# Split weights of a transformer kernel at 160 instead of 192 modulo 256 bytes

## The chip, the cores and the metric

One core of a Trainium2 chip runs the whole program. The metric is the device time of one execution in microseconds; three runs of the kernel before gave a median of 2162.12 us (2159.3 to 2169.41).

## The reference

The reference applies two blocks to one sequence of 256 tokens with 1024 features, all in fp32. The first block has two layers, each a mixer and a convolutional feed-forward part, with RMS norms around both:

```python
x = x + rmsnorm(mixer(rmsnorm(x)))            # layer 0: SSD scan, layer 1: RG-LRU
h = rmsnorm(x, norm_ffn_pre[i])
f = conv_ffn(h, w_up, conv_w, conv_b, w_down)  # 1024 -> 8192 -> gelu(g) * v -> 1024
x = x + rmsnorm(f, norm_ffn_post[i])
```

The second block has two layers of differential attention and a gated delta rule in both directions, merged by gates, and then an MLP with squared ReLU (1024 to 4096 to 1024). Its scales, shifts and gates come from one vector, c, times a matrix of 1024 x 6144 per layer (the "ada" weights). The result must agree with fp32 arithmetic.

## The kernel before

**Layout and tiling.** Activations lie transposed, features on the 128 partitions and the 256 tokens along the free dimension, so every large product has a 128x128 weight matrix as stationary operand and 256 columns of activations as moving operand. All large weights are packed on the host into one stream, w_in, of 263 chunks of 128 x 2048 fp32 (1 MB). A chunk of kind a gives two output tiles of one "unit" (8 matrices each, accumulated over the 1024 inputs); a chunk of kind b takes two input tiles into the 8 accumulators of acc.

**Splitting.** To keep fp32 precision with the fast fp32r format, each weight w is split into w_hi (its rounded copy) and w_lo = w - w_hi, each activation likewise (h_hi and h_lo, or mv_hi and mv_lo). Three products replace one: w_hi * h_hi, w_hi * h_lo, w_lo * h_hi (function three, L484 to L486). ScalarE makes w_hi from raw, half a chunk (128x1024) at a time (act_split, L461); VectorE makes w_lo (dve_split, L468). There are two w_hi and two w_lo tiles, chosen by the parity of the chunk, and three raw tiles.

**Order.** SyncE loads chunk c into raw[c % 3] once chunk c - 3 is split. act_split for a half waits for the load and until TensorE has finished the half that last lay there (semaphore half_done); dve_split waits for act_split (high_parts), and TensorE waits for dve_split (chunk_split). Each half is 24 matmuls, each chunk 48, so 263 chunks are 526 halves and 12624 matmuls. The rest of the program runs between chunks: the stages are, in order, ssd_in (20 chunks), the SSD scan, ssd_out (8), ffn0 (48), lru_in (10), the RG-LRU, lru_out (5), ffn1 (48), and then twice in2 (14), gates (8) with the attention, the delta rule, bra and brb (2 each), out2 (4) and mlp (32). pe_norm (L380) sums squares with fp32 matmuls. The delta rule's fp32 matmuls (L1743 to L1824) work on tiles in ada_ring, tmp, keep and h. In the ffn stages pe_ada (L1318) puts one block of 8 ada products, 384 columns wide, ahead of each chunk of kind b; its results go to misc[0] and misc[1] in turn, and its weights come through two slots of ada_ring, loaded from POOL's queue.

**Memory.** Every tile in SBUF is allocated in order, 128 partitions by so many bytes, each start rounded to 32 bytes. In order and in bytes per partition: raw0 to raw2, x, h, h_hi, h_lo (8192 each), mv_hi, mv_lo (4096 each), par (10088), con (12432), ada_ring (24576), ada_turned (1536), ada_cols (1536), rstd (1024), tmp (4096), cact (32), fold_r (128), ident_r, neg_up_r, cs_parts (512 each), mod (384), gsc (128), keep (43008), weights_offset (128), and then w_hi0, w_hi1, w_lo0, w_lo1 (8192 each). weights_offset is never read or written. With it, w_hi0 starts at 192 modulo 256 bytes; as all four weight tiles are 8192 bytes long, so do the others, and so does every one of the eight 512-byte matrices in a half.

late is a second view of the same bytes: it is allocated at the place of w_hi0 and released at once, so w_hi and w_lo lie over its first 8192 elements. Its 10240 elements hold the SSD scan's tiles while no weights are split (xdt, xdtd, btok, cb, e, e2, st, tok), and its last 2048 elements, above the weights, hold lru_out's w8, attention's rot and the delta rule's kt and vt.

Of the kernel before, what the change touches and what calls it, by code (L numbers as in the profile page):

```python
# [25 lines left out]
P = 128  # L26
# [232 lines left out]
def build(nc, x_in, w_in, gates_in, ada_in, par_in, con_in, out):  # L259
# [7 lines left out]
    with ctx:  # L267
        def sb(name, shape, dtype=f32):
            return ctx.enter_context(nc.sbuf_tensor(name, shape, dtype))
# [32 lines left out]

        keep_cols, late_cols = 10752, 10240
        keep = sb("keep", [P, keep_cols])
        sb("weights_offset", [P, 32])
        with nc.sbuf_tensor("late", [P, late_cols], f32) as late:
            pass
        w_hi = [sb(f"w_hi{i}", [P, CW], f32r) for i in range(2)]
# [1970 lines left out]
```

## Time and profile before

| | us |
|---|---|
| median of three runs | 2162.12 (2159.3 to 2169.41) |
| the profiled execution | 2163.65, of which the profile's span is 2162.0 |
| TensorE busy, matmuls | 1986.0 (92%), 15973 records |
| TensorE busy, weight loads | 1874.7 (87%) |
| VectorE busy | 1339.4 (62%) |
| ScalarE busy | 1010.2 (47%) |
| DMA | 154 GB/s over the span |
| mean granted TensorE clock | 0.953 of full speed |

How to read it: a matmul is recorded from its issue to its end, and several are in flight, so records overlap. The time from one start to the next is the pace of the stream, and the record's own length (276 to 285 ns) is not. In the names of a group, the tile left of the arrow is written, the first one right of it is the moving operand and the second one the stationary operand. An fp32 matmul leaves two records, an fp32r matmul one.

### The profile page before, as it was taken

How to read it: one execution, taken by the hardware profiler on the slowest of the kernel's cores; microseconds unless marked ns; L12 is line 12 of the kernel's file. 1: busy time of each engine (PE TensorE's matmuls, PEld its weight loads, DVE VectorE, ACT ScalarE, POOL GpSimd, SP SyncE). 2: the span in 40 equal slices, each digit the busy share in tenths (PEclk: the TensorE clock that was granted, in tenths of full speed). 3: DMA queues.
4: the chain of work that ended last, by engine and by line, in shares of the span. 5: the costliest groups of instructions: out<-in, count | busy, mean ns of one | idle time of the engine just before them, and what ended most of it. 6: DMA issues, size and time to landing. Idle time of an engine off the chain costs nothing.

```text
span 2162.0 us, 39527 instructions
## 1 busy us (share of the span) xinstructions
PE 1986.0 (92%) x15973; PEld 1874.7 (87%) x15973; DVE 1339.4 (62%) x2017; ACT 1010.2 (47%) x1490; POOL 17.2 (1%) x36
## 2 busy tenths in 40 slices
PE   7989989999896799999799999889989998988998
PEld 6977979999785699999689888889988898888998
DVE  5836576776574676667567655555555765555555
ACT  5644555555457455555455520344445552034443
POOL 0000000000000000000000000000000000000000
PEclk9997999999987899999899999999999999999999
DMA  7530447667532267676233400235543340023553
GB/s 281 181 117 1 176 175 262 256 257 257 210 136 85 98 244 262 262 261 229 83 131 145 154 1 1 98 126 192 191 173 117 137 157 20 1 79 117 195 192 120
DMA packets 43885, 333.98 MB, mean 154 GB/s; under 512 B 4864, under 2 KB 4992, under 8 KB 5504
## 3 DMA queue, kind: packets, MB, share of 16 engines
q1 hardware_dynamic: 38592, 277.89, 35.3%
q0 software_dynamic: 4608, 50.33, 6.3%
q10 hardware_dynamic: 576, 4.19, 0.5%
q8 instruction: 82, 1.34, 0.2%
q14 instruction: 27, 0.22, 0.0%
HBM read 331.35 MB, written 1.05 MB: 154 GB/s over the span
## 4 chain that ended last, share of the span: by engine, by line
PE 84%; DVE 9%; ACT 5%; issue 2%; DMA 0%; DVEq 0%; ACTq 0%
PE unit L484 14%; PE unit L485 14%; PE unit L486 14%; PE acc L484 8%; PE acc L485 7%; PE acc L486 7%; PE misc L380 2%; PE acc L1778 2%; PE misc L1318 2%; PE unit L1771 2%; PE misc L1782 2%; DVE w_lo L468 1%; ACT w_hi L461 1%; PE acc L1381 1%; DVE tmp L1562 1%
## 5 line engine op out<-in xcount | busy, mean ns | idle before, releaser
L468 DVE TENSOR_TENSOR w_lo<-raw,w_hi 128x1024 fp32r<-128x1024 f32 x526 | 640.4, 1225 | 483.8 <-ACT w_hi L461 473.6
L461 ACT ACTIVATE w_hi<-raw 128x1024 fp32r<-128x1024 f32 x526 | 555.1, 1060 | 676.0 <-PE unit L486 404.3
L484 PE MATMUL unit<-h_hi,w_hi 128*128 128x256 f32 x2656 | 756.2, 285 | 47.1 <-DVE h_lo L395 32.4
L485 PE MATMUL unit<-h_lo,w_hi 128*128 128x256 f32 x2656 | 748.0, 282 | 0.0
L486 PE MATMUL unit<-h_hi,w_lo 128*128 128x256 f32 x2656 | 747.7, 282 | 0.0
L484 PEld LDWEIGHTS unit<-h_hi,w_hi 128*128 128x128 f32 x2656 | 512.1, 193 | 57.2 <-issue 40.9
L485 PEld LDWEIGHTS unit<-h_lo,w_hi 128*128 128x128 f32 x2656 | 510.4, 192 | 0.2
L486 PEld LDWEIGHTS unit<-h_hi,w_lo 128*128 128x128 f32 x2656 | 509.0, 192 | 0.0
L484 PE MATMUL acc<-mv_hi,w_hi 128*128 128x256 f32 x1360 | 386.3, 284 | 36.3 <-DVE mv_lo L540 36.3
L485 PE MATMUL acc<-mv_lo,w_hi 128*128 128x256 f32 x1360 | 381.8, 281 | 0.0
L486 PE MATMUL acc<-mv_hi,w_lo 128*128 128x256 f32 x1360 | 381.5, 281 | 0.0
L484 PEld LDWEIGHTS acc<-mv_hi,w_hi 128*128 128x128 f32 x1360 | 260.9, 192 | 57.0 <-DVE mv_lo L540 38.2
L485 PEld LDWEIGHTS acc<-mv_lo,w_hi 128*128 128x128 f32 x1360 | 260.5, 192 | 0.0
L486 PEld LDWEIGHTS acc<-mv_hi,w_lo 128*128 128x128 f32 x1360 | 259.3, 191 | 0.0
L380 PE MATMUL misc<-h,con 128*128 128x256 f32 x192 | 64.2, 505 | 36.9 <-ACT h L367 36.7
L380 PEld LDWEIGHTS misc<-h,con 128*128 128x128 f32 x192 | 48.9, 262 | 50.4 <-ACT h L367 30.4
L1847 ACT ACTIVATE h<-acc 128x512 f32<-128x512 f32 x4 | 2.4, 597 | 169.8 <-PE acc L1800 169.8
L536 ACT ACTIVATE mv_hi<-keep 128x512 fp32r<-128x512 f32 x93 | 57.4, 619 | 41.6 <-DVE keep L934 13.5
L540 DVE TENSOR_TENSOR mv_lo<-keep,mv_hi 128x512 fp32r<-128x512 f32 x93 | 63.5, 687 | 14.5 <-ACT mv_hi L536 14.2
L990 ACT ACTIVATE keep<-unit,par 128x256 f32<-128x256 f32 x128 | 64.2, 550 | 0.0
L1771 PE MATMUL unit<-ada_ring,keep 128*128 128x128 f32 x384 | 53.8, 296 | 9.1 <-DVE ada_ring L1910 9.1
L1043 DVE SCALAR_TENSOR_TENSOR keep<-unit,par,keep 128x254 f32<-128x254 f32 x128 | 55.8, 478 | 8.4
(311 smaller groups left out, 2038.8 us busy)
## 6 DMA issues: line engine op xcount, KB each, us to landing
raw<-w_in SPq DMA_DIRECT2D x263, 1024.0 KB, 4.8
ada_ring<-ada_in POOLq DMA_DIRECT2D x32, 1536.0 KB, 8.5
con<-con_in ACTq DMA_DIRECT2D x1, 1424.0 KB, 6.5
keep<-gates_in ACTq DMA_DIRECT2D x1, 1280.0 KB, 5.6
par<-par_in ACTq DMA_DIRECT2D x1, 1261.0 KB, 14.8
x<-x_in SPq DMA_DIRECT2D x1, 1024.0 KB, 5.9
out<-x SPq DMA_DIRECT2D x4, 256.0 KB, 2.3
con<-con_in ACTq DMA_DIRECT2D x1, 130.0 KB, 6.0
```

The source lines that it names most:

```text
L380: last = mm(misc[0][:, 0:T], ones, h[:, t, :], start=(t == 0), stop=(t == 7))
L461: act(half(w_hi, c, k), raw[c % RAW][:, CW // 2 * k:CW // 2 * (k + 1)], ACT.Copy).then_inc(S("high_parts"), 1)
L468: tt(half(w_lo, c, k), raw[c % RAW][:, CW // 2 * k:CW // 2 * (k + 1)], half(w_hi, c, k).bitcast(f32), ALU.subtract).then_inc(S("chunk_spli ...
L484: mm(out, w, m, start=first, stop=False)
L485: mm(out, w, ml, start=False, stop=False)
L486: return mm(out, wl, m, start=False, stop=last)
L536: act(mv_hi[:, b % 2, :, :], src, ACT.Copy).then_inc(S("mv_hi_done"), 1)
L540: tt(mv_lo[:, b % 2, :, :], src, mv_hi[:, b % 2, :, :].bitcast(f32), ALU.subtract).then_inc(S("mv_ready"), 1)
L990: ins = act(fc[:, s], unit[u % 2][:, s], ACT.Identity, bias=column(u, 4 * side + 3, i), scale=column(u, 4 * side + 2, i))
L1043: ins = stt(fc[:, o + 2:o + T], src[:, o:o + T - 2], column(u, 4 * side, i), fc[:, o + 2:o + T], ALU.mult, ALU.add)
L1318: ins = mm(misc[n % 2][g:g + 32, 0:ADA_W], cact[:, k:k + 1].to_broadcast([P, 32]), ada_slot[n % 2][:, k, :], start=(k < 4), stop=(k >= 4))
L1771: ins = mm(unit[c][:, P * hd:P * (hd + 1)], W["lt"][:, c, hd, :], W["t"][:, c, hd, :], start=True, stop=True)
```

## The change

The spacer ahead of late and the weights becomes 24 instead of 32 elements per partition, 96 instead of 128 bytes. w_hi0, w_hi1, w_lo0, w_lo1 and late start 32 bytes lower, at 160 modulo 256 bytes. Nothing else is different.

```diff
@@ -302,7 +302,7 @@
 
         keep_cols, late_cols = 10752, 10240
         keep = sb("keep", [P, keep_cols])
-        sb("weights_offset", [P, 32])
+        sb("weights_offset", [P, 24])
         with nc.sbuf_tensor("late", [P, late_cols], f32) as late:
             pass
         w_hi = [sb(f"w_hi{i}", [P, CW], f32r) for i in range(2)]
```

## Rows read from the trace of the kernel before

**Rows 1.** The page, part 4: the chain that ended last, by engine and by line.

```profile
PE 84%; DVE 9%; ACT 5%; issue 2%; DMA 0%; DVEq 0%; ACTq 0%
PE unit L484 14%; PE unit L485 14%; PE unit L486 14%; PE acc L484 8%; PE acc L485 7%; PE acc L486 7%; PE misc L380 2%; PE acc L1778 2%; PE misc L1318 2%; PE unit L1771 2%; PE misc L1782 2%; DVE w_lo L468 1%; ACT w_hi L461 1%; PE acc L1381 1%; DVE tmp L1562 1%
```

**Rows 2.** The page, part 5: costliest groups of instructions (columns named in the line above).

```profile
L468 DVE TENSOR_TENSOR w_lo<-raw,w_hi 128x1024 fp32r<-128x1024 f32 x526 | 640.4, 1225 | 483.8 <-ACT w_hi L461 473.6
L461 ACT ACTIVATE w_hi<-raw 128x1024 fp32r<-128x1024 f32 x526 | 555.1, 1060 | 676.0 <-PE unit L486 404.3
L484 PE MATMUL unit<-h_hi,w_hi 128*128 128x256 f32 x2656 | 756.2, 285 | 47.1 <-DVE h_lo L395 32.4
...
L484 PE MATMUL acc<-mv_hi,w_hi 128*128 128x256 f32 x1360 | 386.3, 284 | 36.3 <-DVE mv_lo L540 36.3
```

**Rows 3.** The waits: engine, tile, line, whom it waited for, us, times, longest.

```profile
ACT w_hi L461 <- PE unit L486: 404.3, 275, 8.9
ACT w_hi L461 <- PE acc L486: 270.4, 159, 5.8
...
PE acc L484 <- DVE mv_lo L540: 36.3, 7, 21.0
PE unit L484 <- DVE h_lo L395: 32.4, 16, 4.7
```

**Rows 4.** Timeline of TensorE in ssd_in: start us, us, engine, line, instruction.

```profile
56.25 0.28 PE L484 MATMUL unit<-h_hi,w_hi 128*128 128x256 f32 x1
...
59.08 0.28 PE L484 MATMUL unit<-h_hi,w_hi 128*128 128x256 f32 x1
```

**Rows 5.** Timeline of TensorE in mlp_0, the same columns.

```profile
1481.02 0.28 PE L486 MATMUL acc<-mv_hi,w_lo 128*128 128x256 f32 x1
1481.13 0.28 PE L484 MATMUL unit<-h_hi,w_hi 128*128 128x256 f32 x1
...
1483.85 0.28 PE L484 MATMUL unit<-h_hi,w_hi 128*128 128x256 f32 x1
```

**Rows 6.** Windows: busy us and records of each engine, clock, DMA share, GB/s.

```profile
core 0: us, PE busy (x) PEld busy (x) DVE busy (x) ACT busy (x) POOL busy (x), PEclk, DMA share, GB/s
60.00:80.00 20.00, 20.00 (x172) 20.00 (x171) 17.80 (x29) 13.65 (x24) 0.00 (x0) 1.00 0.48 166
...
331.00:347.00 16.00, 16.00 (x139) 15.49 (x142) 10.84 (x17) 7.59 (x10) 0.00 (x0) 1.00 0.77 287
351.00:363.00 12.00, 12.00 (x108) 12.00 (x108) 7.88 (x12) 6.86 (x9) 0.00 (x0) 1.00 0.76 292
1460.00:1600.00 140.00, 140.00 (x1237) 140.00 (x1237) 78.83 (x78) 68.28 (x79) 0.00 (x0) 1.00 0.54 191
```

**Rows 7.** One line's instructions (L1782, L1749): ns min/median/max.

```profile
L1782 PEld LDWEIGHTS misc<-tmp,ada_ring x320: 192/192/333, 1263.6 to 1896.8; 128*128 128x128 f32 x160
L1782 PE MATMUL misc<-tmp,ada_ring x320: 274/275/421, 1263.8 to 1896.9; 128*128 128x128 f32 x160
...
L1749 PE MATMUL misc<-keep x64: 275/275/275, 1245.4 to 1858.6; 128*128 128x128 f32 x64
```

**Rows 8.** The same view of L1844, L1436 (ScalarE) and L901 (VectorE).

```profile
L1844 ACT ACTIVATE ada_ring<-ada_ring x8: 1040/1042/1057, 1252.0 to 1804.2; 128x1024 f32<-128x1024 f32 x8
...
L1436 ACT ACTIVATE h<-h x8: 1041/1052/1061, 1115.5 to 1726.9; 128x1024 f32<-128x1024 f32 x8
...
L901 DVE TENSOR_TENSOR late<-late x8: 1217/1224/1226, 160.1 to 206.3; 128x1024 f32<-128x1024 f32 x8
```

**Rows 9.** Timelines of ScalarE and VectorE in mlp_0, with the idle time before.

```profile
1462.29 1.06 ACT L461 ACTIVATE w_hi<-raw 128x1024 fp32r<-128x1024 f32 x1 [1.14 <-PE unit L486]
1465.01 1.06 ACT L461 ACTIVATE w_hi<-raw 128x1024 fp32r<-128x1024 f32 x1 [1.66 <-PE unit L486]
...
1463.39 1.23 DVE L468 TENSOR_TENSOR w_lo<-raw,w_hi 128x1024 fp32r<-128x1024 f32 x1 [0.89 <-ACT w_hi L461]
```

**Rows 10.** Timeline of TensorE in in2_0, an fp32 group of 256 columns.

```profile
1109.57 3.62 PE L1381 MATMUL acc<-h,con 128*128 128x256 f32 x16
```

## The prediction

> **What bounds the kernel now.** I read the chain that ended last first. TensorE holds 84% of it, and 64% of the span (14 + 14 + 14 + 8 + 7 + 7) lies on the three lines that multiply by the split weights [rows 1]. The costliest groups say the same: 2656 matmuls of each of three kinds into unit and 1360 of each into acc, beside 526 half-chunk splits on ScalarE (L461) and 526 on VectorE (L468) [rows 2]. Both splitters wait for TensorE or for each other, not TensorE for them: ScalarE waited 404.3 + 270.4 us for matmuls, VectorE 473.6 us for ScalarE [rows 2], and the largest waits of a matmul for the other engines are 32 to 36 us each, at stage starts [rows 3]. So the time moves if a matmul's pace moves, and hardly otherwise.
>
> Then I read the timeline of TensorE for that pace, and it has two. In ssd_in, 24 starts from 56.25 to 59.08 us are 117.9 ns apart [rows 4]. In mlp_0, 24 starts from 1481.13 to 1483.85 us are 113.3 ns apart [rows 5]. The granted clock is 1.00 at both, the shapes and tiles are the same. From the starts in ns the paces are 117.78 and 113.33; the difference of 4.44 ns is the price I use. The reader can find it again in the windows [rows 6]: 20 us hold 172 matmul records at the slow pace (two of them cut by the edges: 20 / 170 = 117.6 ns), 140 us hold 1237 at the quick one (140 / 1235 = 113.4 ns).
>
> A stretch keeps its pace from beginning to end and changes it only after an interruption. Counting the timeline by half chunks of 24 matmuls, 517 of 526 can be read (the others are at the half clock): 199 slow, 318 quick. Slow are 20 halves of ssd_in, all 16 read of ssd_out, 93 of the two ffn stages, 3 of lru_out, 37 of the two in2 and 30 of bra, brb and out2; quick are all 126 read of the mlp stages, all 32 of gates, 97 of ffn, and 63 of the remaining stages. In ffn the pace alternates: slow after the ada block into misc[0], quick after the one into misc[1] (the two ffn windows in rows 6: 16 us with 139 records, 12 us with 108). VectorE, ScalarE and DMA shares don't separate the two: mlp is quick with DMA at 0.54, ffn is quick at 0.76 and slow at 0.77 [rows 6]. So the pace is a phase between the stream of weight loads and the stream of moving columns, which the entry to a stretch picks; whether addresses enter into it, no row tells directly.
>
> **The change, part by part.** The spacer shrinks from 128 to 96 bytes per partition. No instruction, wait, queue or transfer is added, removed or reordered. Five tiles start 32 bytes lower: w_hi0, w_hi1, w_lo0, w_lo1 and late. From the tile sizes, w lies 78112 bytes above ada_ring, 49440 above tmp, 125248 above h_hi, 108864 above mv_hi, 43136 above keep and 90560 above con; with w at 192 modulo 256 before, ada_ring and tmp are at 160, h_hi, mv_hi and h at 128, keep at 64, con at 0. The new place, 160, is thus one that ada_ring and tmp already have, and every other place in this list is a multiple of 64.
>
> *Matmuls with w as stationary operand.* Removed 0, added 0; what can change is the pace of 12624 of them (263 chunks of 48). The nearest rows with a stationary tile at 160 are the 320 records of L1782, moving operand tmp and weights ada_ring, both at 160: median 275 ns a record and 192 a weight load, the smallest there is too. The same shape from keep at 64 (L1749) has median 275 [rows 7]. So a tile off the 64-byte grid costs TensorE nothing there. These are plain fp32 and 128 columns wide, not the 256-column fp32r stream, so they bound the level of a pace, not which of two a stretch takes. I take 0 for the level. For the choice, the ends are every stretch quick, 199 x 24 x 4.44 ns = 21.2 us less, and every stretch slow, 318 x 24 x 4.44 ns = 33.9 us more. I take 0 here too, as the single likeliest, because in the rows a change of operands alone (h_hi into mv_hi, unit into acc, [rows 5]) never switches the pace; interruptions do, and these stay.
>
> *Splits.* ScalarE's 128x1024 pass over ada_ring at 160 took 1042 ns median, over h at 128 took 1052 [rows 8]; the present split takes 1060 [rows 2]. VectorE's 128x1024 on late, itself at 192 now, took 1224 [rows 8], the split 1225. No sign of a price. The cover, if there is one: in mlp a split starts every 2.72 us, takes 1.06 us on ScalarE and 1.23 on VectorE and follows an idle time of 0.89 to 1.66 us [rows 9], so some 0.4 us more on each is hidden. Without cover, the 10% that separate nothing here would be 0.1 us x the few splits at stage starts, under 2 us. Taken: 0.
>
> *Other users of late* (SSD's decay tiles, the attention and delta tiles kt, vt, rot, and lru_out's w8): some hundred instructions on the path, with the same tile classes as above. Taken: 0; ends -1 and +1 us, from 8 passes of 1224 ns [rows 8] at 10%.
>
> *DMA.* No transfer writes to w or late; raw stays. 0.
>
> Sum: 2163.65 us for the profiled execution (span 2162.0) + 0. That execution lies 1.5 us above the median of the three runs, 2162.12, which runs from 2159.3 to 2169.41. The forecast is on the median's scale: 2162.
>
> One rule of the skill would say otherwise. The rows have starts 113.33 and 117.78 ns apart for 256 columns. The Trainium skill, TensorE: Matmul & The Clock Gate, section "Wait — 56ns, not 53.3ns?", gives back-to-back warm matmuls N / 2.4 GHz plus about 2.5 ns, that is 109.2 ns for 256; here no such matmul ran at that pace, and an estimate by that page would put the whole kernel near 2090 us if both paces fell to it (7632 x 4.2 ns + 4776 x 8.6 ns = 73 us less).
>
> **The rivals.**
> *A, more stretches slow (ends slower).* If the relative address of weights (192, then 160) and moving operand (128) is part of what locks the phase, a new address redraws the stretches. More are quick than slow now, so a redraw more often costs: at even odds, 258.5 - 199 = 59.5 halves x 24 x 4.44 ns = +6.3 us, 2168. It decides once 101 halves (10.8 us) turn slow; mlp alone has 126 and is one uninterrupted stretch per block, so mlp turning slow gives +13.4 us, 2176; everything slow gives 2196. For: the pace sits on the exact pair of streams that the change shifts, and mlp's 126 halves hang on two entries. Against: h_hi and mv_hi, hi and lo alike, never switch it; L1782 shows no price at 160.
>
> *B, more stretches quick.* The same lock, other draws: the 93 slow ffn halves turning quick give -9.9 us, 2152; all 199 give 2141. For: ffn alternates at every entry, so little seems to hold it. Against: only 199 halves can gain, 318 can lose.
>
> *C, a new pace.* Weight loads of 512 bytes per matrix that start in the middle of a 64-byte piece touch nine such pieces, not eight. If each cost one more 64-byte step of reading, 16 clocks of 2.4 GHz or 6.67 ns, exposed on every matmul: 12408 x 6.67 ns = +83 us, 2245. Against: L1782's loads do just this and last 192 ns, no longer than their own minimum [rows 7]. The opposite, a pace without the stall: the fp32 matmuls of 256 columns have 16 records in 3.62 us, 216 ns each [rows 10]; half a record, 108 ns, is the lowest that a row lets one think of, and gives 7632 x 5.3 ns + 4776 x 9.8 ns = 87 us less, 2075. This is the side on which the page's 109.2 ns lies.
>
> *D, the change does nothing.* If the allocator rounded to 64 bytes, nothing would move: 2162. But ada_ring starts at 160, a multiple of 32 and not of 64, so I expect 96 bytes to stay 96.
>
> **How the numbers follow.** Forecast (paces stay where they are) 0.38 and D 0.03; A 0.34, of which 0.28 beyond 10.8 us; B 0.20, of which 0.18 beyond; C slower 0.03, C quicker 0.02. Half a per cent, 10.8 us, is about what a measurement of this kernel can tell from no change (the three runs spread over 10). Slower by more: 0.28 + 0.03 = 0.31. Faster by more: 0.18 + 0.02 = 0.20. Within: 0.38 + 0.03 + 0.06 + 0.02 = 0.49. The range goes to B's end, 2141, and to A up to mlp slow plus a part of ffn, 2188 (A's full end 2196 and both sides of C are left out, under 2 in 10). The likeliest case alone: 2158 to 2168.
>
> **What the profile after would show.** Right: 24 starts in ssd_in's first half chunks still 2.83 us, in mlp 2.72 us, and 172 and 1237 records in the same windows; means of L461 and L468 at 1060 and 1225; L1782 unchanged. Rival A: mlp's 24 starts take 2.83 us and the stage of 32 chunks grows by 6.7 us. Rival B: ffn's pairs all at 2.72. Rival C: a figure that is neither 113.3 nor 117.8. Wrong altogether if the time moves while both paces and their stretches stay, or if a new wait for the splits shows ahead of L484.

## The result: slower by 1.7%

The kernel with the weights at 160 modulo 256 bytes ran at a median of 2202.73 us (four runs, 2201.54 to 2203.32), against 2165.76 us for the kernel before beside it (2159.3 to 2170.7). The ratio is 1.0172, with a 95% interval of 1.014 to 1.0204. The forecast was 2162 us, no change, with a range up to 2188.

The instructions of every engine, and their order, are the same; the span grew from 2162.0 to 2201.5 us. First the page's groups that answer to those of [rows 2]:

```profile
span 2201.5 us, 39527 instructions
...
L468 DVE TENSOR_TENSOR w_lo<-raw,w_hi 128x1024 fp32r<-128x1024 f32 x526 | 640.3, 1224 | 522.7 <-ACT w_hi L461 512.7
L461 ACT ACTIVATE w_hi<-raw 128x1024 fp32r<-128x1024 f32 x526 | 555.6, 1061 | 713.9 <-PE unit L486 427.1
L484 PE MATMUL unit<-h_hi,w_hi 128*128 128x256 f32 x2656 | 763.7, 288 | 46.5 <-DVE h_lo L395 32.6
...
L484 PE MATMUL acc<-mv_hi,w_hi 128*128 128x256 f32 x1360 | 391.6, 288 | 35.6 <-DVE mv_lo L540 35.6
```

The two splits kept their length to a nanosecond (1224 and 1061 ns), so the new place costs ScalarE and VectorE nothing. They are idle longer, 713.9 us instead of 676.0 and 522.7 instead of 483.8, because ScalarE waits longer for TensorE and VectorE for ScalarE. TensorE waits for the others as little as before (46.5 and 35.6 us). What grew is the mean length of a matmul's record, 285 to 288 ns.

The timeline of TensorE shows by how much they moved apart. These are 24 starts in ssd_in (compare [rows 4]) and 24 in mlp_0 (compare [rows 5]):

```profile
56.30 0.28 PE L484 MATMUL unit<-h_hi,w_hi 128*128 128x256 f32 x1
...
59.14 0.28 PE L484 MATMUL unit<-h_hi,w_hi 128*128 128x256 f32 x1
...
1500.07 0.28 PE L484 MATMUL acc<-mv_hi,w_hi 128*128 128x256 f32 x1
...
1502.91 0.28 PE L484 MATMUL unit<-h_hi,w_hi 128*128 128x256 f32 x1
```

Both take 2.84 us, 118.3 ns a matmul, where they took 2.83 and 2.72 us. The window view says it over a long stretch of mlp_0, to set beside the last line of [rows 6]:

```profile
1500.00:1600.00 100.00, 100.00 (x847) 100.00 (x847) 53.72 (x53) 46.23 (x53) 0.00 (x0) 1.00 0.53 188
```

That is 100 us with 845 starts, 118.3 ns; before it was 113.4. Over all the half chunks that can be read the quick pace is gone: none runs at 113.3, and nearly all run between 118.1 and 118.5 ns, mean 118.29. Eight half chunks of in2 still run at 117.8; they come back below. A few single ones beside an interruption have 117.9 to 118.0. In the working of the prediction, 7632 quick matmuls lose 118.29 - 113.33 = 4.96 ns each, 37.9 us, and 4776 at the 117.8 ns pace 0.51 ns, 2.4 us: 40.3 us, of which the span shows 39.5. No other place has to be looked for. The fp32 line whose operands lie at 160, L1782, did not change (see [rows 7]). It could not have: the change moves neither tmp nor ada_ring.

```profile
L1782 PEld LDWEIGHTS misc<-tmp,ada_ring x320: 192/192/333, 1279.3 to 1926.3; 128*128 128x128 f32 x160
L1782 PE MATMUL misc<-tmp,ada_ring x320: 274/275/421, 1279.5 to 1926.4; 128*128 128x128 f32 x160
```

### The profile page after: what moved, and what is told of

It reads as the page before. It is cut to its first block, busy times and chain, and to the rows that moved or that the text cites. A ratio compares the mean times of both kernels' runs of the same rounds, so it can differ in the third digit from the quotient of the medians.

```text
span 2201.5 us, 39527 instructions
## 1 busy us (share of the span) xinstructions
PE 2027.9 (92%) x15973; PEld 1915.9 (87%) x15973; DVE 1339.6 (61%) x2017; ACT 1010.9 (46%) x1490; POOL 17.2 (1%) x36
## 4 chain that ended last, share of the span: by engine, by line
PE 85%; DVE 8%; ACT 4%; issue 2%; DMA 1%; DVEq 0%; ACTq 0%
PE unit L484 15%; PE unit L485 14%; PE unit L486 14%; PE acc L484 8%; PE acc L485 7%; PE acc L486 7%; PE acc L1778 2%; PE misc L380 2%; PE misc L1318 2%; PE unit L1771 2%; PE misc L1782 2%; ACT w_hi L461 1%; DVE w_lo L468 1%; PE acc L1381 1%; DVE tmp L1562 1%
## 5 line engine op out<-in xcount | busy, mean ns | idle before, releaser
L468 DVE TENSOR_TENSOR w_lo<-raw,w_hi 128x1024 fp32r<-128x1024 f32 x526 | 640.3, 1224 | 522.7 <-ACT w_hi L461 512.7
L461 ACT ACTIVATE w_hi<-raw 128x1024 fp32r<-128x1024 f32 x526 | 555.6, 1061 | 713.9 <-PE unit L486 427.1
L484 PE MATMUL unit<-h_hi,w_hi 128*128 128x256 f32 x2656 | 763.7, 288 | 46.5 <-DVE h_lo L395 32.6
L485 PE MATMUL unit<-h_lo,w_hi 128*128 128x256 f32 x2656 | 756.1, 285 | 0.0
L486 PE MATMUL unit<-h_hi,w_lo 128*128 128x256 f32 x2656 | 755.5, 284 | 0.0
L484 PE MATMUL acc<-mv_hi,w_hi 128*128 128x256 f32 x1360 | 391.6, 288 | 35.6 <-DVE mv_lo L540 35.6
L485 PE MATMUL acc<-mv_lo,w_hi 128*128 128x256 f32 x1360 | 387.1, 285 | 0.0
L486 PE MATMUL acc<-mv_hi,w_lo 128*128 128x256 f32 x1360 | 386.7, 284 | 0.0
```

The lines of the kernel that those rows point to most:

```text
L461: act(half(w_hi, c, k), raw[c % RAW][:, CW // 2 * k:CW // 2 * (k + 1)], ACT.Copy).then_inc(S("high_parts"), 1)
L468: tt(half(w_lo, c, k), raw[c % RAW][:, CW // 2 * k:CW // 2 * (k + 1)], half(w_hi, c, k).bitcast(f32), ALU.subtract).then_inc(S("chunk_spli ...
L484: mm(out, w, m, start=first, stop=False)
L485: mm(out, w, ml, start=False, stop=False)
L486: return mm(out, wl, m, start=False, stop=last)
```

## The experiments

Three theories stood after that. G, the grid: a stationary operand that doesn't start on a multiple of 64 bytes costs time. R, the distance: what counts is how far apart, modulo 256, the stationary and the moving operand start (64 before, 32 after; the distances here are the stationary operand's start less the moving one's). L, the draw: each address redraws the phase by chance.

### Other places, and the moving operand moved instead

Two kernels change the spacer alone, and two move h_hi, h_lo, mv_hi and mv_lo with spacers around them that leave everything else in place modulo 256:

```diff
# e1_w224
+        sb("weights_offset", [P, 40])
# e2_w128
+        sb("weights_offset", [P, 16])
# e3_moving160: weights_offset stays [P, 32]
+        sb("moving_offset", [P, 8])
         h_hi = sb("h_hi", [P, DT_, T], f32r)
...
+        sb("par_offset", [P, 56])
         par = sb("par", [P, NPAR])
# e4_both_lower: weights_offset is [P, 24]
+        sb("moving_offset", [P, 56])
         h_hi = sb("h_hi", [P, DT_, T], f32r)
...
+        sb("par_offset", [P, 8])
         par = sb("par", [P, NPAR])
```

> Spacer 40 instead of 32 elements: the weight tiles at 224 modulo 256, off the 64-byte grid on the other side. Theory G (a stationary operand that does not start on a multiple of 64 bytes costs time on every matmul): one pace of 118.3 ns everywhere, 2198 to 2206 us. Theory R (the distance between stationary and moving operand decides; it was 64, is 32 after the change): here the distance is 96, so a pace that need not be 118.3; if the 32-byte distance alone is bad, near 2163 us. Theory L (a redraw of the phase by chance at each address): any mix of 113.3 and 117.8 ns, 2141 to 2196 us.

> Spacer 16 elements: the weight tiles at 128 modulo 256, on the 64-byte grid, distance 0 to the moving operands. Theory G: two paces, 113.3 and 117.8 ns, as before; 2141 to 2196 us, most likely 2150 to 2175. Theory R: the pace changes, to one that neither kernel had, up or down. Theory L: a mix of the two paces, another than before.

> The weight tiles stay at 192, while h_hi, h_lo, mv_hi and mv_lo start 32 bytes higher, at 160 modulo 256: now the moving operand is off the 64-byte grid and the distance is 32 as after the change. Theory G for weight loads alone: the two paces stay and the time is 2155 to 2175 us. Theory G for either operand, and theory R: 118.3 ns everywhere, near 2202 us.

> The weight tiles at 160 as after the change, and h_hi, h_lo, mv_hi, mv_lo 32 bytes lower as well, at 96 modulo 256, so the distance is 64 as before the change. Theory R: the two paces come back, 2155 to 2175 us. Theory G: 118.3 ns everywhere or slower, 2198 us or more.

| kernel | weights at | moving at | distance | median us | ratio to before (95%) |
|---|---|---|---|---|---|
| the change | 160 | 128 | 32 | 2202.73 | 1.0172 (1.014 to 1.0204) |
| e1_w224 | 224 | 128 | 96 | 2201.92 | 1.017 (1.0114 to 1.0227) |
| e2_w128 | 128 | 128 | 0 | 2222.06 | 1.0257 (1.0202 to 1.0312) |
| e3_moving160 | 192 | 160 | 32 | 2203.81 | 1.0173 (1.0119 to 1.0228) |
| e4_both_lower | 160 | 96 | 64 | 2160.24 | 0.9988 (0.9957 to 1.0018) |

E4 settles it: the weights lie where the change puts them, at 160 modulo 256 and off the 64-byte grid, the moving tiles are off it too, and all of the loss is gone. E3 is the mirror of it: the weights stay at 192 and the loss is there in full, at a pace of 118.2 to 118.5 ns like the change's. G falls, and so does G's hope for 128 (e2, on the grid, is the slowest so far). R stands; e1, at distance 96, has paces of 117.2 to 118.9 ns. A line of the window view of each in mlp, e4, e3 and e2 in that order:

```profile
1460.00:1590.00 130.00, 130.00 (x1149) 130.00 (x1148) 72.15 (x71) 63.18 (x72) 0.00 (x0) 1.00 0.54 192
```

```profile
1500.00:1600.00 100.00, 100.00 (x848) 100.00 (x847) 53.87 (x54) 45.67 (x52) 0.00 (x0) 1.00 0.53 185
```

```profile
1500.00:1620.00 120.00, 120.00 (x1002) 120.00 (x1001) 63.15 (x64) 54.74 (x63) 0.00 (x0) 1.00 0.52 184
```

Taking two records off for the edges, they are 113.3, 118.2 and 120.0 ns.

E4 is not the kernel before to the letter. Its span is 2152.7 us, 9.3 below, with the same two paces but 118 slow half chunks instead of 199: all of ffn but one half chunk is quick. 81 x 24 x 4.44 ns = 8.6 us. So theory L has its part in which of the two paces a stretch takes. It may account for the spread of the kernel before, 2151.54 to 2175.71 us in the 13 runs beside these four and up to 2183.58 in a later set, where the change, with one pace nearly throughout, stays within 2 us; that was not followed run by run.

The kernel has a check of the distance built in. In the last two chunks of each in2, 192 matmuls in all, w is the moving operand and h_hi or h_lo the stationary one, against what is said of every large product ahead of the prediction. There the distance is 128 - 160 = -32, that is 224, in the changed kernel. These are 24 of its starts in in2_0:

```profile
1181.96 0.28 PE L484 MATMUL unit<-w_hi,h_hi 128*128 128x256 f32 x1
...
1184.79 0.28 PE L484 MATMUL unit<-w_hi,h_hi 128*128 128x256 f32 x1
```

They take 2.83 us, in ns 117.8 a matmul; e3, also at 224 there, has 116.7 in in2_0 and 117.8 in in2_1. The last map below has these two paces at 224 (117.8, 116.7, 117.8, 116.7), and 118.3 at 32. So the direction of the distance counts, and the same bytes cost differently when the operands change roles.

### The rest of the places in steps of 64, and w_lo alone

```diff
# e5_w0
+        sb("weights_offset", [P, 48])
# e6_w64
+        sb("weights_offset", [P, 64])
# e7_lo_alone (late and split_cols 56 elements longer)
+        sb("lo_offset", [P, 56])
         w_lo = [sb(f"w_lo{i}", [P, CW], f32r) for i in range(2)]
# e8_lo_pair: as e7, and h_lo and mv_lo each between spacers of 56 and 8 elements
+        sb("h_lo_offset", [P, 56])
         h_lo = sb("h_lo", [P, DT_, T], f32r)
+        sb("h_lo_end", [P, 8])
```

> Spacer 48 elements: the weight tiles at 0 modulo 256, distance 128 to the moving operands. If the pattern repeats every 128 bytes: 120.0 ns on every matmul and 2222 us, like distance 0. If every 256: another pace, anything from 109 to 120 ns, 2090 to 2222 us. If it repeats every 64 bytes, distance 64 would have run like distance 0, which it did not.

> Spacer 64 elements: the weight tiles at 64 modulo 256, distance 192. If the pattern repeats every 128 bytes: the two paces, 113.3 and 117.8 ns, and 2150 to 2175 us. If every 256: another pace.

> w_hi stays at 192, w_lo alone starts 32 bytes lower modulo 256, at 160. Every product but the third keeps its distance of 64, w_lo and h_hi of the third stand 32 apart, and so do w_lo and h_lo, which is the pair whose weight load and columns lie beside each other in time. Each load paying for its own distance: two thirds at the old paces, one at the new, near 2175 us. One locked phase that a single bad pair spoils: near 2202 us.

> w_lo, h_lo and mv_lo all 32 bytes lower modulo 256, the hi tiles where they were. In time, the load of w_lo lies beside the columns of h_lo (distance 64 as before), and both loads of w_hi beside the columns of h_hi (64 as before). Within one product the distances are now 96 (w_hi with h_lo) and 32 (w_lo with h_hi). Theory P (what meets is the next weight load and the running columns): as the kernel before, both paces 113.3 and 117.8 ns, 2150 to 2175 us. If the two operands of one product meet: as e7 or worse, 2175 to 2202 us.

E5 (distance 128): 2212.32 us, ratio 1.0214 (1.0153 to 1.0275), with stretches at 118.5 to 118.9 and others at 120.0 ns. E6 (distance 192): 2194.93 us, 1.0133 (1.0072 to 1.0194), the same two paces as before, but 498 half chunks slow and 21 quick. Distance 0 ran everything at 120.0 ns and 192 isn't like 64 in its draws, so the pattern doesn't repeat after 128 bytes.

E7 moves one operand of three: 2204.05 us, 1.018 (1.0142 to 1.0217), as slow as moving all. No half chunk is quick; the paces are 117.8 to 118.1 in some stretches and 119.7 to 120.3 in others. The theory that a load pays for its own distance (2175 us) fails; the time is that of the other one, a locked phase that one operand out of step spoils. E8 restores the distances between what lies side by side in time (the load for the next matmul and the columns of the running one) and breaks them inside a product: 2196.17 us, 1.0136 (1.01 to 1.0173), 117.7 to 118.0 ns everywhere. Theory P falls in its strict form: no quick pace came back. Which reads meet which is left open.

### TensorE alone: a map of the distances

Four small kernels have no splits, no weight stream and no other engine at work while the streams run. Each fills one moving pair and stationary tiles, and runs the hi-hi, hi-lo, lo-hi pattern on views of the stationary tiles that start a chosen number of bytes further, modulo 256, than the moving tiles:

```python
w[d] = t[:, d // 4:d // 4 + 2048]
for d in PLACES:
    for entry in range(3):
        ...
        for s, m in ((wh, m_hi), (wh, m_lo), (wl, m_hi)):
            ins = mm(ps[0][:, 0:T], s[:, j, :], m[:, j, :], ...)
```

> A kernel that does none of the reference's work but TensorE streams: for 16 distances from 0 to 240 bytes, in steps of 16, between the start of the stationary and of the moving operand modulo 256, three streams of 96 matmuls each in the kernel's hi-hi, hi-lo, lo-hi pattern, with three different entries, and no ScalarE, VectorE or DMA work beside them. Theory R (two read streams of TensorE meet, by their distance): 113.3 or 117.8 ns at 64, 118.2 to 118.5 at 32 and 96, 120.0 at 0, and a curve in between that repeats or not beyond 128. If other engines' accesses were part of it, all 16 distances run at one pace here.

> The map kernel with 16 other distances: 4, 8, 24, 40, 52, 56, 60, 68, 72, 76, 184, 196, 200, 204, 212, 216 bytes. The first map had 113.3 ns, for the entry from idle, at 64 and 192 alone, 117.8 for the other entries there, 116.7 at 208. If the quick pace needs an exact distance, none here has it; if it has a width of some bytes, 56 to 72 have it. If 16 bytes are the grain of the reads, 52, 56 and 60 equal 48 and 68, 72 and 76 equal 64.

The window view of the first map, 8 us inside a stream: distances 0, 32, 64 after an fp32 product of 256 columns (slow), 64 after one of 128 columns and a wait (quick), 112, 192 after the same as the last (quick) and 208. The third entry, four products of 384 columns and a wait, was slow at 64 and 192 too:

```profile
55.00:63.00 8.00, 8.00 (x69) 8.00 (x69) 0.00 (x0) 0.00 (x0) 1.00 0.01 2
...
133.00:141.00 8.00, 8.00 (x70) 8.00 (x70) 0.00 (x0) 0.00 (x0) 1.00 0.01 2
...
211.00:219.00 8.00, 8.00 (x70) 8.00 (x69) 0.00 (x0) 0.00 (x0) 1.00 0.00 0
223.00:231.00 8.00, 8.00 (x73) 8.00 (x72) 0.00 (x0) 0.00 (x0) 1.00 0.01 2
...
328.00:336.00 8.00, 8.00 (x69) 8.00 (x68) 0.00 (x0) 0.00 (x0) 1.00 0.00 0
...
536.00:544.00 8.00, 8.00 (x73) 8.00 (x72) 0.00 (x0) 0.00 (x0) 1.00 0.01 2
562.00:570.00 8.00, 8.00 (x71) 8.00 (x70) 0.00 (x0) 0.00 (x0) 1.00 0.00 0
```

With ScalarE and VectorE at 0.00, the paces of the full kernels are all here: 120.0 ns at 0, 118.3 at 32, 113.3 or 117.8 at 64 and 192, so two operands of TensorE itself make them. The starts in ns tell paces apart that give a window of 8 us the same count of matmuls. The last map took every distance in steps of 4 bytes, four entries each; the table has the mean over the last 36 starts of each stream of 48:

> All 64 distances in steps of 4 bytes, four streams of 48 matmuls each: entered from idle, after one fp32 product of 128 columns, after the 8-product ada block, after one of 256 columns. From the two maps: 113.3 ns from every entry at 52, from some at 64, 76, 192 and 196, nowhere below 113.3; 115.6 at 8; 116.7 to 120 elsewhere. If the page's 109.2 ns is to be had, some distance shows it.

| distance | ns per matmul, by entry (idle, fp32 128, ada block, fp32 256) |
|---|---|
| 0 | 120.0 four times |
| 8 | 115.6 four times |
| 28 | 116.7 four times |
| 32 | 118.3 118.3 118.3 118.4 |
| 52 | 113.3 four times |
| 56 | 117.8 four times |
| 64 | 117.8 113.3 117.8 113.3 |
| 76 | 113.3 113.3 120.0 113.3 |
| 88 | 113.3 113.3 113.3 120.0 |
| 108 | 122.2 122.2 122.2 120.0 |
| 192 | 113.3 117.8 117.8 117.8 |
| 208 | 120.0 116.7 116.7 116.7 |
| 224 | 117.8 116.7 117.8 116.7 |

Seven of the 64 distances (52, 64, 76, 88, 168, 180, 192) have a quick entry at all in it. The fine map had 52 quick at all three entries and 76 at two of three; 196, which the expectation above calls quick, ran at 117.8 to 118.3 ns in both maps. None runs below 113.3 ns; all the others lie between 115.6 and 123.3. The curve is not smooth: 4 bytes beside 52 it is 117.8 to 123.3. The guess of a 16-byte grain in the second expectation is wrong.

The entries, with streams at four distances one after the other:

> Streams of 48 matmuls at distances 64, 192, 208 and 32, entered from idle, after 8 or 16 or 7 fp32 products of 384 columns (the ada block is 8), and after one or two fp32 products of 128 columns. Theory F (an fp32 block flips the phase of the stream): at 64 and 192 the pace alternates between 113.3 and 117.8 ns from stream to stream after each 8-block, and stays after 16. Theory I (only an entry from idle is quick): 113.3 after idle, 117.8 after every block. At 208 and 32 one pace whatever the entry.

At 64 an 8-product block flips the pace, each time but the first, which follows two quick streams from idle and leaves the next one quick. Here are the first and the last start, 36 matmuls apart, of the four streams that follow such blocks:

```profile
50.57 0.28 PE L98 MATMUL stream<-m_lo,w_above 128*128 128x256 f32 x1
...
54.65 0.28 PE L98 MATMUL stream<-m_lo,w_above 128*128 128x256 f32 x1
...
61.53 0.28 PE L98 MATMUL stream<-m_lo,w_above 128*128 128x256 f32 x1
...
65.77 0.28 PE L98 MATMUL stream<-m_lo,w_above 128*128 128x256 f32 x1
...
72.65 0.28 PE L98 MATMUL stream<-m_lo,w_above 128*128 128x256 f32 x1
...
76.73 0.28 PE L98 MATMUL stream<-m_lo,w_above 128*128 128x256 f32 x1
...
83.60 0.28 PE L98 MATMUL stream<-m_lo,w_above 128*128 128x256 f32 x1
...
87.84 0.28 PE L98 MATMUL stream<-m_lo,w_above 128*128 128x256 f32 x1
```

4.08, 4.24, 4.08 and 4.24 us: 113.3, 117.8, 113.3, 117.8 ns. That is like the alternation of the ffn stages before, and the bank into which the block writes plays no part (the next four, into another bank, alternate alike). But theory F was right by half: 16 products flip as well, one fp32 product of 128 columns flips, two don't, and 7 products don't. At 192 it doesn't alternate: quick after idle, then slow after every block, and in the end slow after idle too. At 208 and 32 there is one pace whatever the entry in this run, though the last map has 120.0 at 208 from idle. Nor does a block of 8 flip the pace wherever the distance is 64: e4 has the same ada blocks between its streams in ffn and stays quick, but for one half chunk of 188. What else decides is open.

### A version at distance 52

```diff
-        sb("weights_offset", [P, 32])
+        sb("weights_offset", [P, 24])
...
-        w_hi = [sb(f"w_hi{i}", [P, CW], f32r) for i in range(2)]
-        w_lo = [sb(f"w_lo{i}", [P, CW], f32r) for i in range(2)]
+        w_hi = [sb(f"w_hi{i}", [P, CW + 64], f32r)[:, 5:5 + CW] for i in range(2)]
+        w_lo = [sb(f"w_lo{i}", [P, CW + 64], f32r)[:, 5:5 + CW] for i in range(2)]
```

The tile late and the constant split_cols are 256 elements longer, to make room.

> The weights start at 180 modulo 256 (the spacer of the changed kernel, and views that skip 5 elements of tiles 64 elements longer), distance 52 to the moving operands. In the fine map distance 52 ran at 113.3 ns from all three entries. If the kernel's streams follow the map, all 517 half chunks are quick: 2162 - 21 = 2141 us, 2138 to 2145. If starts off the 32-byte grid cost ScalarE or VectorE something, or the entries of the kernel reach another lock, 2150 to 2205.

Ten runs have a median of 2159.62 us (2147.62 to 2164.05), a ratio of 0.9973 (0.9949 to 0.9997): a shade faster than before, not the 21 us hoped for. Off the 32-byte grid the splits took 1063 and 1227 ns, as before within 3. The streams follow the map in most of the kernel, all but 5 half chunks of ffn quick, 399 in all. But the execution profiled also entered ssd_out and the whole of mlp_0 in a lock at 120.0 ns that the map's four entries never met, while mlp_1 was quick. Its windows in mlp_0 and mlp_1:

```profile
1430.00:1590.00 160.00, 160.00 (x1335) 160.00 (x1335) 85.77 (x85) 72.76 (x85) 0.00 (x0) 1.00 0.52 183
2000.00:2140.00 140.00, 140.00 (x1238) 140.00 (x1237) 78.68 (x77) 67.52 (x78) 0.00 (x0) 1.00 0.53 188
```

The same code, operands and addresses modulo 256, 120.0 and 113.3 ns: the entry alone differs. A stretch like that costs 64 halves x 24 x 6.67 ns = 10.2 us, and all 110 slow half chunks up to 17.6 of the 21 us. How to enter every stretch quick was not tried in the full kernel.

## Why the prediction was wrong, point by point

**What bounds the kernel, right.** TensorE's pace was the thing to price; the splits, the other users of late and the DMA moved nothing, as costed. The time came wholly from the pace of 12408 matmuls.

**"So a tile off the 64-byte grid costs TensorE nothing there ... I take 0 for the level": this step failed.** The sentence on the grid was even true: in e4 a tile at 160 costs nothing. The error was to read an address where a distance was at work. The row at hand, L1782, has both operands at 160, so its distance is 0, and it is plain fp32, a stream whose pace no run here changed. It bounded neither end. And it was read by the length of its records, 275 and 192 ns, which is not the pace. The weight loads show how blind that is; these are the same line before and after the change:

```profile
L485 PEld LDWEIGHTS unit<-h_lo,w_hi 128*128 128x128 f32 x2656 | 510.4, 192 | 0.2
L485 PEld LDWEIGHTS unit<-h_lo,w_hi 128*128 128x128 f32 x2656 | 511.0, 192 | 0.2
```

192 ns both times, while the starts of the quick stretches moved from 113.3 to 118.3 ns apart. The two kinds of row that the argument had, one distance (64) in fp32r and another kind of matmul, could not carry a level of 0 for distance 32. In the place of 0 the runs show +4.96 ns where the pace was 113.3 and +0.51 where it was 117.8.

**"A change of operands alone never switches the pace": true and misleading.** h_hi and mv_hi stand at the same place modulo 256, and so do the hi and lo tiles. The rows varied everything but the one quantity that the change alters.

**Rival A named the right cause with the wrong shape.** It had the relative address in it, and the sign, but thought that a new address deals the same two paces anew, with everything slow at 2196 as its end. That end exists, at distance 192: e6, 2194.93 us. The change gave a third pace just above the slow one, which no stretch with w as the stationary operand escapes. Redraws exist: e4, e6 and e9 are redraws. At distance 32 there is nothing to draw.

**Rival C expected a new pace, which came, and for a reason that is refuted.** Nine pieces instead of eight would cost at any place off the 64-byte grid; e4 costs nothing there, and e2, on the grid, costs most. Its size, +6.67 ns on every matmul, was too large: the mean went from 115.0 (from the prediction's own counts) to 118.3. The quick side of C, below 113.3 ns, exists at no distance of the map; the 109.2 ns worked out from the Trainium skill (TensorE: Matmul & The Clock Gate) were not seen for fp32r pairs with a new weight load each, at 64 distances and four entries.

**The range.** It ended at 2188 because the ends were built from two paces and cut at 8 in 10; with all of A's end it would have been 2196, and the result lies nearly 7 us beyond even that. A range for an unseen placement needed the bound of a third pace, and the only one at hand had 0.03. Most of the probability for no change came from the missing price.

## What to carry to other kernels

Where TensorE alternates weight loads and matmuls without a gap, as in these streams of fp32r with 256 columns, the start addresses of both operands modulo 256 bytes belong to the tuning: here the pace varied from 113.3 to 123.3 ns with nothing else changed. Other types and widths were not measured. Treat the distance as the variable, not the alignment, and measure the candidates, since the neighbours of a good one say nothing about it. And compare the pace stretch by stretch with starts in the timeline, for a stream can have two paces at one distance, chosen by how it was entered, and then single runs spread.

## What the runs showed of the hardware that was not expected

Two read streams of TensorE disturb each other by their addresses, with no other engine at work: 120.0 ns at distance 0, 118.3 at 32, 113.3 at best, for 256 columns at a granted clock of 1.00. The Trainium skill, SBUF — State Buffer, section "Who interferes with whom", gives TensorE two independent read ports, one for the moving operand and one for the weight load, and says that it never waits on anyone. The maps don't agree in so far as the pace of the two together depends on their distance; whether it is the port, the memory behind it or the order in which the engine issues them, no run here tells apart.

A stream locks into a pace and keeps it: mlp_0 before has 113.3 ns over 63 half chunks, some 1500 matmuls, and e9 120.0 over the same stretch. One fp32 product of 128 columns between two streams can change the pace of the 48 matmuls that follow, and did so each of five times at distance 64.
